# The delta-rule head loop with its output transposes, mask products and row work in another order

## The reference, cut to what matters

```python
def chunk_gated_delta_rule(q, k, v, g, beta):
    gc = jnp.cumsum(g, axis=-1)
    decay = jnp.where(tril, jnp.exp(jnp.where(tril, gc[..., :, None] - gc[..., None, :], 0.0)), 0.0)
    lower = jnp.where(strict, einsum('nik,njk->nij', k * beta, k) * decay, 0.0)
    t_inv = triangular_solve(eye + lower, eye)          # unit lower triangle, inverted
    u, w = t_inv @ (v * beta), t_inv @ (k * beta * exp(gc))
    intra = jnp.where(tril, einsum('nik,njk->nij', q, k) * decay, 0.0)
    # scan over chunks: v_new = u - w @ state; o = (q*exp(gc)) @ state + intra @ v_new
    #                   state = state * exp(gc_last) + (k*exp(gc_last-gc)).T @ v_new

def gated_deltanet_branch(qkv, z, ...):
    qkv = silu(centred_depthwise_conv(qkv, conv_w))     # 5 taps, then q, k, v per head
    q, k = l2_norm(q), l2_norm(k)
    o = delta_rule(forward) + flip(delta_rule(flipped)) # two directions, d = 0 and 1
    return rms_norm(o, o_gain) * silu(z)
```

## Time and profile before

| | |
|---|---|
| median of three runs | 2807.88 us |
| the profiled execution, its own time | 2807.88 us |
| its span in the trace | 2806.1 us |
| TensorE busy | 2667.6 us, 95% |
| weight loads (beside it) | 1988.8 us, 71% |
| VectorE, ScalarE, GpSimd busy | 35%, 29%, 28% |
| share of the chain of waits on TensorE | 82% |
| the eight turns of the head loop | about 84 to 612 us of the span |

### The profile page before, as it was taken

One profiled execution on the slowest core, in us unless ns is written; L12 is line 12 of the kernel. 1 busy time (PEld: TensorE's weight loads), 2 busy tenths in 40 slices (PEclk: granted clock), 3 DMA queues, 4 the chain that ended last, 5 costly groups with the idle time before them and its releaser, 6 DMA issues.

```text
span 2806.1 us, 35476 instructions
## 1 busy us (share of the span) xinstructions
PE 2667.6 (95%) x14496; PEld 1988.8 (71%) x14496; DVE 993.0 (35%) x1800; ACT 823.4 (29%) x1439; POOL 786.4 (28%) x633
## 2 busy tenths in 40 slices
PE   7999999999899996999999799999999999999998
PEld 4777777885458883444444497888888897988887
DVE  3565566533422133221212477420011587300012
ACT  2444443332432221000000325532222327322222
POOL 2222233310114400000000152434445442444454
PEclk8999999999999997999999999999999999999999
DMA  7212222012113325999999621222322221232231
GB/s 263 53 60 68 85 64 60 30 35 68 35 35 123 106 87 206 371 409 409 409 408 408 255 91 61 63 88 90 99 96 90 91 76 46 79 102 90 92 103 45
DMA packets 212566, 382.39 MB, mean 136 GB/s; under 512 B 10834, under 2 KB 145878, under 8 KB 211414
## 3 DMA queue, kind: packets, MB, share of 16 engines
q1 hardware_dynamic: 211088, 379.06, 37.9%
q10 hardware_dynamic: 1349, 1.51, 0.2%
HBM read 378.44 MB, written 2.10 MB: 136 GB/s over the span
## 4 chain that ended last, share of the span: by engine, by line
PE 82%; DMA 9%; DVE 4%; ACT 3%; issue 1%; DVEq 1%; SPq 0%; ACTq 0%; POOL 0%; PEld 0%; PEldq 0%
PE bank L1563 14%; PE bank L1567 14%; PE bank L1568 14%; PE bank L1823 6%; PE bank L1331 5%; DMA ring<-in_w_up 4%; DMA ring<-in_w_gate 3%; PE bank L1768 2%; PE bank L1365 2%; PE bank L1711 2%; PE bank L1427 2%; PE bank L1436 1%; PE bank L1617 1%; PE bank L1440 1%; PE bank L1346 1%
## 5 line engine op out<-in xcount | busy, mean ns | idle before, releaser
L680 POOL TENSOR_TENSOR w_lo<-ring,w_hi 128x512 fp32r<-128x512 f32 x448 | 604.9, 1382 | 1495.3 <-ACT w_hi L728 1495.3
L728 ACT ACTIVATE w_hi<-ring 128x2048 fp32r<-128x2048 f32 (+1 forms) x114 | 215.0, 1886 | 677.2 <-PE bank L1563 677.1
L1563 PE MATMUL bank<-hT_hi,w_hi 128*128 128x512 f32 (+1 forms) x928 | 356.3, 384 | 3.2 <-DVE hT_lo L2614 1.6
L1567 PE MATMUL bank<-hT_lo,w_hi 128*128 128x512 f32 (+1 forms) x928 | 351.8, 379 | 0.0
L1568 PE MATMUL bank<-hT_hi,w_lo 128*128 128x512 f32 (+1 forms) x928 | 348.5, 376 | 0.0
L1823 PE MATMUL bank<-ring,xeT 128*64 128x512 f32 x992 | 225.5, 596 | 30.9 <-DMA ring<-in_w_gate 18.8
L1563 PEld LDWEIGHTS bank<-hT_hi,w_hi 128*128 128x128 f32 x928 | 174.8, 188 | 39.5 <-DVE conv_acc L2712 2.4
L1568 PEld LDWEIGHTS bank<-hT_hi,w_lo 128*128 128x128 f32 x928 | 174.6, 188 | 35.8
L1567 PEld LDWEIGHTS bank<-hT_lo,w_hi 128*128 128x128 f32 x928 | 174.1, 188 | 31.9 <-issue 1.0
L1823 PEld LDWEIGHTS bank<-ring,xeT 128*64 128x64 f32 x992 | 77.2, 136 | 155.6 <-issue 153.1
L2805 DVE TENSOR_TENSOR ffn_hT<-ffn_sg,bank 128x512 f32<-128x512 f32 x44 | 30.2, 687 | 423.0 <-PE bank L1568 423.0
(11 more groups left out here) (490 smaller groups left out, 4854.9 us busy)
## 6 DMA issues: line engine op xcount, KB each, us to landing
ring<-in_w_gate SPq DMA_DIRECT2D x86, 1024.0 KB, 9.1
ring<-in_w_down SPq DMA_DIRECT2D x86, 1024.0 KB, 14.1
ring<-in_w_up SPq DMA_DIRECT2D x82, 1024.0 KB, 14.1
ring<-in_w_in SPq DMA_DIRECT2D x33, 1024.0 KB, 5.4
head_w<-in_w_in SPq DMA_DIRECT2D x32, 512.0 KB, 5.4
mod_w<-in_w_mod SPq DMA_DIRECT2D x8, 2048.0 KB, 7.9
ring<-in_w_out SPq DMA_DIRECT2D x12, 1024.0 KB, 4.9
ring<-in_w_mod SPq DMA_DIRECT2D x8, 1024.0 KB, 15.9
```

The costliest lines, as they stand in the source:

```text
L680: last = pool.tensor_tensor(w_lo[m % 2][:, cs], src[:, cs], w_hi[m % 2][:, cs].bitcast(F32), ALU.subtract)
L728: return act.activation(dst, src, ACT.Copy)
L1563: first = mm(dst, a[0], b[0], start=start, stop=False)
L1567: mm(dst, a[0], b[1], start=False, stop=False)
```

## The change

On TensorE, the transposes of v stand behind the gate sums, not ahead of q's lengths, and the wait for `head_done` moves to the first projection. The output transposes move from before the mod2 products to the end of the turn, after them, and write bank 1. On VectorE `o_ready` is given after the mod2 bank is copied. Both q_decT products stand ahead of the decay products, and the two `intra` products move from level 3 of the solve to the place between `l_ready` and the identity step. On ScalarE the silu of v and of z move from the end of a turn to the start of the next, and the copy of the transposed k stands between the two directions' decays. On GpSimd level 1 of `solve_S` follows level 0 at once. SyncE's list is unchanged.

```diff
@@ pool
                 pool.wait_ge(sem("l_ready"), h + 1)
                 level(0)
+                level(1)
                 in_turn(pool, "k_tok_ready", h)
                 in_turn(pool, "v_tok_ready", h)
                 pool.wait_ge(sem("eye_ready"), h + 1)
-                level(1)
                 level(2)
@@ act
-            def take_z(h):
+            def head(h, more):
+                convolved(h, 2)
                 act.wait_ge(sem("z_done"), h + 1)
                 act.activation(flat_rows(z_silu[:]), bank[2][:], ACT.Silu).then_inc(once_a_turn["z_ready"], 1)
-
-            def head(h, more):
                 act.wait_ge(sem("tok_done"), h * 2 + 1)
...
                     act.activation(flat_rows(decay[:, d]), flat_rows(decay[:, d]), ACT.Exp, scale=-1.0).then_inc(sem("decay_ready"), 1)
-                act.wait_ge(sem("kT_done"), h + 1)
-                copy(knT[:], bank[4][:]).then_inc(sem("kT_ready"), 1)
+                    if d == 0:
+                        act.wait_ge(sem("kT_done"), h + 1)
+                        copy(knT[:], bank[4][:]).then_inc(sem("kT_ready"), 1)
...
-                if more:
-                    convolved(h + 1, 2)
-                    in_turn(act, "o_ready", h)
-                    take_z(h + 1)
-                else:
+                if not more:
                     keep_cq(3)
@@ pe
                 if s == 0 and k0 == 0:
                     pe.wait_ge(sem("qkv_w_in"), h * 48 + 48)
-                    pe.wait_ge(sem("raw_ready"), h * 3)
+                    pe.wait_ge(sem("head_done"), h)
...
                 to_tokens(1, 4)
-
-                pe.wait_ge(sem("head_done"), h + 1)
-                to_tokens(2, 5)
                 pe.wait_ge(sem("q_sq_ready"), h + 1)
...
                     last.then_inc(sem("gc_row_done"), 1)
+                to_tokens(2, 5)
                 fill(0, 0, KD)
...
                 if more:
                     project_z(h + 1)
-                    turn_o()
                 else:
                     latent_q(3)
...
                 pe.drain().then_inc(sem("mod2_done"), 1)
                 if not more:
                     latent_kv(0)
-                    turn_o()
+                pe.wait_ge(sem("raw_ready"), h * 3 + 6)
+                in_turn(pe, "o_ready", h)
+                for t in range(TT):
+                    last = pe.transpose(bank[1][:, tiles[t]], o_tok[:, t, :], ident[:])
+                last.then_inc(once_a_turn["oT_done"], 1)
@@ dve
-                for d, dst in enumerate((l_neg, l_bwd)):
+                for d in range(2):
                     dve.wait_ge(sem("e_row_ready"), h * 2 + d + 1)
                     tt(q_decT[:, d, :], conv_out[:, 0, :], e_row[:, d, :], ALU.mult).then_inc(sem("q_dec_ready"), 1)
+                for d, dst in enumerate((l_neg, l_bwd)):
                     dve.wait_ge(sem("decay_ready"), h * 2 + d + 1)
...
                 tt(flat_rows(l_neg[:]), flat_rows(l_neg[:]), bank[3][:], ALU.mult).then_inc(sem("l_ready"), 1)
+                in_turn(dve, "kq_done", h)
+                dve.wait_ge(sem("intra_masked"), h * 2 + 2)
+                for d in range(2):
+                    last = tt(flat_rows(intra[:, d]), flat_rows(intra[:, d]), bank[5][:], ALU.mult)
+                last.then_inc(once_a_turn["intra_ready"], 1)
                 dve.wait_ge(sem("S_ready"), h * 7 + 1)
...
-                dve.drain().then_inc(once_a_turn["o_ready"], 1)
+                dve.drain()
                 dve.wait_ge(sem("mod2_done"), h + 1)
                 copy(mod2_part...).then_inc(once_a_turn["mod2_copied"], 1)
+                dve.drain().then_inc(once_a_turn["o_ready"], 1)
```

More of the change, by code:

```diff
@@ L364, in build @@
             "head_vector": (
-                "head_q_ready", "g_wide_ready", "k_tok_ready", "intra_ready", "o_ready", "mod2_copied",
+                "head_q_ready", "g_wide_ready", "k_tok_ready", "intra_ready", "mod2_copied", "o_ready",
             ),
@@ L893, in head @@
                 in_turn(act, "oT_done", h)
-                act.activation(oT_dn[:, h:h + 1, :].rearrange("p a n -> p (a n)") if isinstance(h, int) else oT_dn[:, bass.ds(h, 1), :].rearrange("p a n -> p (a n)"), bank[5][:], ACT.Copy,
+                act.activation(oT_dn[:, h:h + 1, :].rearrange("p a n -> p (a n)") if isinstance(h, int) else oT_dn[:, bass.ds(h, 1), :].rearrange("p a n -> p (a n)"), bank[1][:], ACT.Copy,
                                scale=cols_a[:, R_OG:R_OG + 1]).then_inc(sem("head_done"), 1)
@@ L903, in _ @@
             q_squared()
-            convolved(0, 2)
-            take_z(0)
             with act.Fori(0, HEADS - 1) as h:
@@ L1340, in latent_q @@
                         arrived(pe, N_LATENT + 1)
-                        pe.wait_ge(sem("raw_ready"), HEADS * 3)
+                        pe.wait_ge(sem("head_done"), HEADS)
                     if t == 2:
@@ L1512, in turn_latent @@
                 last.then_inc(sem("latent_turned"), 1)
-            in_turn(pe, "mod2_copied", HEADS - 1)
             gate_rows(0)
@@ L2288, in head @@
                         conv(h + 1, (lv - 1) // 3, *i)
-                    if lv == 3:
-                        in_turn(dve, "kq_done", h)
-                        dve.wait_ge(sem("intra_masked"), h * 2 + 2)
-                        for d in range(2):
-                            last = tt(flat_rows(intra[:, d]), flat_rows(intra[:, d]), bank[5][:], ALU.mult)
-                        last.then_inc(once_a_turn["intra_ready"], 1)
                 dve.wait_ge(sem("TT_done"), h * 7 + 7)
```

## The result

The changed kernel took 2854.97 us (median of four runs, 2853.17 to 2857.24) and the kernel before 2809.97 us beside it. The ratio is 1.0167, with a 95% interval of 1.0154 to 1.0179: slower by 1.5% to 1.8%. It takes in all 15 executions of the changed kernel on record (2853.17 to 2861.08 us, median 2857.22), so it is a little above the ratio of the two medians given first. I had forecast 2847.5 us with a range of 2831 to 2854. The direction and the price of the waits were right, that of the clock was not, and the time lies 0.97 us above the range.

The account below looks back on a forecast made before the run. TensorE, busy 64.35 of 65.12 us a turn, was taken as the bound. Border 6.2, path to the solve 23.8 and clock 9.6 made 39.6 us on 2807.9: 2847.5 us, range 2831 to 2854.

Parts of the forecast that it names:

- The border: Between two turns of TensorE's head loop: the next turn starts 0.88 us later, at seven borders 6.2 us.
- My lower bound of 0.44: Between two turns: the loop's branch is wholly hidden, so the next turn starts 0.44 us later.
- ScalarE's longer start: Start of ScalarE's turn: everything behind comes 3 us later, covered by TensorE's work with 1.0 us to spare; cost nothing.
- The path to the solve: From k's transposes to TensorE's solve: TensorE stands still 2.98 us in each of eight turns, 23.8 us.
- K: In each turn, the end of TensorE's transposes of the normed k; 225.58 in the trace before the change.
- Rival 2: VectorE's identity step slips in between GpSimd's levels 0 and 1: stall 1.93 us, 2829.5 us, up to 2836; chance 0.13.
- Sum of the waits: TensorE's waits in the head loop: 6.2 us between turns plus 23.8 us ahead of the solve.
- The clock: After the wait ahead of the solve, TensorE runs at half clock for 3.4 us: 1.6 us in six turns, 9.6.
- My upper bound: Half clock after the wait ahead of the solve, in all eight turns in full: 13.6 us.
- Rival 1: TensorE's clock stays up throughout, so only the waits are paid: 2837.9 us; chance 0.18.
- Rival 3: ScalarE, not TensorE, becomes the bound before K: 0.3 to 1 us more in seven turns, 2850 to 2855; chance 0.08.
- Rivals 4 and 5: 4: not slower, `eye_ready` by K + 6.94, 2810-2813, 0.05. 5: ScalarE late anyway, forecast within 1 us, inside the 0.55.

Follow-up runs that it names:

- the border undone: Changed kernel with the output transposes ahead of mod2 again and `o_ready` ahead of the copy of mod2's bank: 2837.63 us, ratio 1.0104.
- both fillers: Changed kernel plus matrix products with overwritten results, one ahead of the output transposes and three ahead of the solve: 2841.07 us, ratio 1.0113.
- all three together: Changed kernel with level 1 after `eye_ready`, k's copy after both decays and output transposes ahead of mod2: 2809.84 us, ratio 0.9998.

## Why the prediction missed its range

In the order of its steps, with what the runs showed:

- *The border, 0.88 a turn.* The direction was right, the size 0.37 too high. From the start of the z projection to the next turn's first transposes it is 220.59 - 209.84 = 10.75 after, and 214.51 - 204.27 = 10.24 in the same view before: 0.51. With the border undone the turn without a fall is 0.48 shorter (68.32 against 68.80), which agrees.

```profile
204.27 7.31 PE L1365 MATMUL bank<-head_w,hT 128*128 128x128 f32 x64
...
214.51 1.09 PE L1377 MATMUL bank<-ident,conv_out 128*128 128x128 f32 x8 [0.64 <-issue]
```

  Counted from the end of the scan, as I had counted (204.44 before, 210.00 after), mod2 ends at 9.00 and the output transposes start at 10.09, both as forecast to 0.02. The wait for the copy is 1.09. Of the branch I had left 0.44 on the path, and it is wholly hidden: the next transposes start 0.50 after the first output transpose, which is their own time. My lower bound of 0.44 was the right case.
- *ScalarE's longer start, nothing.* Right, with less to spare than the 1.0 forecast. The copy of k sits idle ahead of k's transposes in every turn, for 0.71 us behind the one border without a fall and 2.3 to 2.4 behind one with a fall, so ScalarE waits for TensorE there and not the other way. The Trainium skill (ScalarE: Activation LUTs, What ACT_TABLE_LOAD costs) gives some 2.66 us for a switch; by that, as an estimate, 0.4 us a turn would have been lost. The trace has 1.28 for the load and 1.30 from its start to the next activation, and nothing was lost.
- *The path to the solve, 2.98 a turn.* 2.91 measured, and each step came within 0.1 of its forecast. K is 232.70 + 0.60 = 233.30. The copy of k starts at K + 0.04, `l_ready` is given at K + 6.68 (forecast 6.66), level 1 ends at K + 9.25 (9.23), the identity step at K + 9.80 (9.78), and TensorE, free at K + 6.94, starts at K + 9.85 (9.92). The pieces are as said: q_decT and the forward products undisturbed, 2.25 for the backward ones, levels 0 and 1 together 2.49, the identity step 1.73 (forecast 1.7 to 1.8). The Trainium skill (SBUF — State Buffer, SBUF: two separate sides) calls the ports an exclusive lock that goes to whichever starts first; every identity step with level 1 behind it took 1.73 to 1.74, with or without the rest of the change, and 0.69 without it: the trace agrees. In the backward products it fits less well by the starts that the profile gives: VectorE began at 236.19, GpSimd at 236.24, and yet VectorE's first product took 1.46. Rival 2, the step slipping in between the levels, is out.
- *Sum of the waits.* 30.0 forecast. The turn without a fall is 68.80, 3.68 longer: 0.51 at the border, 3.07 at the solve from start to start, and 0.1 in the solve's first group. The 3.07 is 0.16 more than the idle stretch, because in the kernel before the solve's first product starts 0.16 before the filler ahead of it ends. Seven such turns, 2.1 ahead of the first identity step, and behind the last one 1.0 less its fall of 1.2, make 27.7.
- *The clock, "I take it for six of eight turns: 9.6 us".* This is the step that failed. The seven turns hold 41.9 - 7 x 3.68 = 16.1 us for eleven falls; the twelfth, beside the last solve, makes it 17.3 in the loop, where I had put 9.6. One more fall stands 16 us behind the loop and goes with the +2.05 there; I had said that what follows the loop only moves with it. Six falls beside the solve were forecast and six came, at about 1.2 each (71.68 - 70.45). The six at the border were not in the sum at all: I had looked at the clock only beside the longest wait. Each costs 1.65 (70.45 - 68.80). My upper bound, all eight solves in full at 13.6, was for that reason no bound.
- *The criterion behind it* was wrong as well. I judged by the length of the stretch, 2.98 near the 3.13 that had a fall behind it. The runs have 2.90 with no fall in eight turns, 2.90 with a fall in every other turn, and 1.09 with a fall in six of seven. That six falls came beside the solve, as I said, is luck.
- *The account.* Waits 27.7 for 30.0, falls beside the solve 6 x 1.23 = 7.4 for 9.6, falls at the border 6 x 1.65 = 9.9 for nothing, behind the loop 2.05 for nothing: 47.1 in the profiled executions, where 39.6 was forecast. The step over the edge of the range was small, and a part of it lies elsewhere: I had counted from 2807.9, and the kernel before took 2809.97 beside the changed one.
- *Rival 1*, the clock stays up, 2837.9: this is what both fillers made, 2841.07. It was the right price for the waits within 2 us (30.0 against 32). The border undone has nearly the same time, 2837.63, by chance: its waits are fewer. *Rival 3*: wrong in its mechanism, though its band held the time. *Rivals 4 and 5* are out: `eye_ready` is late in every turn, and undoing k's copy alone brings 27 us.

How the chip picks the turns with falls is not settled. The length of a stretch and the work around it don't decide, as two turns of one execution show. What is left is where the turn's idle and thin stretches come to lie in time, and moving them did change the falls: turns of 71.68 have both falls each time, 68.32 none, 69.2 one in every other. Another reading of the last, that a turn is spared after one with a fall, doesn't go with the changed kernel, which has falls in six turns in a row. In the changed kernel the turn grows until it reaches 71.68, and then stays. A rule that gives the falls from a timeline I don't have.

## What to carry to other kernels

Before a wait is put into another engine's chain, count what that chain has to spare (here 1.53 us): what goes beyond it is paid in every turn. If an order adds idle time to the busiest engine, price the clock at every new gap of the loop, the short ones too, and put both "in every turn" and "never" into the range, since neighbouring versions with the same gap had either. Short work in front of a loop's branch hides the branch, as long as nothing new is waited for.

## What was unexpected of the hardware

- Undoing one part of the change moves the clock elsewhere: in the profiled executions the 1.08 us gap at the border had no falls with level 1 undone, and with it in place six. So the parts don't add up: single undoings bring 25, 27 and 18 us by their ratios, 70 in sum, and all three together 47. Each alone takes nearly all falls with it, so that the clock is counted three times. The waits by themselves go the other way: the turns without a fall get 0.75, 0.77 and 0.48 shorter, 2.0 in sum, and 3.66 with all three undone.
- A low clock costs only where TensorE sets the pace: in the run with k's copy undone a fall at the border left the turn at 68.03 us, and the idle time ahead of the solve shrank from 1.50 to 0.51.
- GpSimd holds up other VectorE forms too. In the changed kernel a step of the next head's convolution, a scalar_tensor_tensor, takes 1.60 us beside GpSimd and 0.75 alone; with level 1 undone its tensor_scalar takes 1.17 instead of 0.48, and the wait of 0.45 for solve_X follows behind it.
- After its wait the solve's first group of eight 128x128 products takes 1.16 us, where it takes 1.05 in the full stream of the kernel before, and the next group starts 0.99 behind it instead of 0.89: this wait costs 0.1 us beside itself.
